# One-core transformer block kernel: the compressed branch's weight chunks spread over eight attention steps, and its later pieces moved

## What is computed

```python
def compress(kv, pos_emb, w1, w2):
    blocks = kv[:, idx] + pos_emb            # 31 blocks of 32 tokens, stride 16
    hid = jax.nn.gelu(flat @ w1)             # (31, 2048) @ (2048, 256), for keys and for values
    return hid @ w2                          # 64 columns
...
kc, vc = compress(k_cmp, ...), compress(v_cmp, ...)
kc = apply_rope(kc, ccos, csin)
p_cmp = masked_softmax(einsum(q, kc), valid_c)   # 31 compressed keys
o_cmp = einsum(p_cmp, vc)
out = gates[0] * o_cmp + gates[1] * o_slc + gates[2] * o_win
```

## Time and profile before

| what | value |
|---|---|
| median of 3 runs | 2398.99 us (2395.02 to 2399.94) |
| the profiled execution's own time | 2396.53 us |
| its span in the profile | 2394.7 us |
| share of the span, PE busy | 97% |
| share of the span, DVE busy | 64% |
| share of the span, ACT busy | 38% |
| the attention steps in the profile | 183.94 to 309.55 us |
| step 4, 16, 28 and 36 begin on PE at | 205.21, 230.67, 264.27 and 285.86 us |

### The profile page before, as it was taken

One profiled execution on the slowest core, in us unless ns is written; L12 is line 12 of the kernel. 1 busy time (PEld: TensorE's weight loads), 2 busy tenths in 40 slices (PEclk: granted clock), 3 DMA queues, 4 the chain that ended last, 5 costly groups with the idle time before them and its releaser, 6 DMA issues.

```text
span 2394.7 us, 29589 instructions
## 1 busy us (share of the span) xinstructions
PE 2319.8 (97%) x11200; PEld 1945.8 (81%) x11200; DVE 1525.8 (64%) x2596; ACT 915.8 (38%) x1329; POOL 845.3 (35%) x620
## 2 busy tenths in 40 slices
PE   7989899999999999999999999999999999999996
PEld 6878888888888887788888888888888888888884
DVE  4366667777435766567977764552222788888887
ACT  4336544333325445333323333443222333333332
POOL 0030011221000000000057787886760766666651
PEclk9999999999999999999999999999999999999998
DMA  6222046786332221233366665559676999999993
GB/s 211 77 65 62 1 158 226 268 276 206 105 97 80 88 71 53 93 127 97 118 155 146 146 144 131 119 121 279 146 204 233 324 368 353 343 357 364 358 352 130
DMA packets 205115, 434.21 MB, mean 181 GB/s; under 512 B 54112, under 2 KB 104304, under 8 KB 204464
## 3 DMA queue, kind: packets, MB, share of 16 engines
q1 hardware_dynamic: 81840, 251.79, 30.9%
q0 software_dynamic: 72368, 119.73, 18.5%
q10 hardware_dynamic: 50768, 60.82, 7.4%
HBM read 369.22 MB, written 63.05 MB: 181 GB/s over the span
## 4 chain that ended last, share of the span: by engine, by line
PE 93%; DVE 3%; ACT 1%; DMA 1%; issue 1%; POOL 0%; SPq 0%; DVEq 0%; ACTq 0%
PE PS L266 28%; PE PS L267 28%; PE PS L268 28%; PE PS L2228 1%; PE PS L2328 1%; PE PS L2160 1%; PE PS L410 1%; PE PS L2080 1%; PE PS L2148 1%; PE PS L2306 1%; DMA RAW<-in_w_in 1%; PE PS L2005 1%; DVE PS L1878 0%; DMA RAW<-in_peer_v 0%; PE PS L2014 0%
## 5 line engine op out<-in xcount | busy, mean ns | idle before, releaser
L261 DVE TENSOR_TENSOR WL<-RAW,WH 128x1024 fp32r<-128x1024 f32 (+1 forms) x414 | 505.9, 1223 | 588.1 <-ACT WH L255 558.3
L266 PE MATMUL PS<-HH,WH 128*128 128x512 f32 x1696 | 667.2, 393 | 5.9 <-DVE HL L435 4.3
L268 PE MATMUL PS<-HH,WL 128*128 128x512 f32 x1696 | 660.9, 390 | 0.0
L267 PE MATMUL PS<-HL,WH 128*128 128x512 f32 x1696 | 660.7, 390 | 0.0
L861 POOL DMA_INDIRECT gates<-A,PLACE x256 | 436.7, 1706 | 330.7 <-DVE PLACE L1809 204.9
L255 ACT ACTIVATE WH<-RAW 128x1024 fp32r<-128x1024 f32 (+1 forms) x414 | 434.8, 1052 | 255.2 <-PE PS L268 223.0
L266 PEld LDWEIGHTS PS<-HH,WH 128*128 128x128 f32 x1696 | 318.9, 188 | 73.8 <-issue 5.7
L268 PEld LDWEIGHTS PS<-HH,WL 128*128 128x128 f32 x1696 | 318.6, 188 | 66.6
L267 PEld LDWEIGHTS PS<-HL,WH 128*128 128x128 f32 x1696 | 319.0, 188 | 65.5 <-issue 1.0
L266 PE MATMUL PS<-WH,WGH 128*128 128x512 f32 x768 | 299.1, 389 | 4.6 <-DVE WGL L1862 3.9
L267 PE MATMUL PS<-WL,WGH 128*128 128x512 f32 x768 | 298.8, 389 | 0.0
(11 more groups left out here) (351 smaller groups left out, 2747.8 us busy)
## 6 DMA issues: line engine op xcount, KB each, us to landing
RAW<-in_peer_u SPq DMA_DIRECT2D x128, 512.0 KB
RAW<-in_peer_v SPq DMA_DIRECT2D x128, 512.0 KB
A<-in_w_ada POOLq DMA_DIRECT2D x48, 512.0 KB, 4.6
A<-gates ACTq DMA_DIRECT2D x32, 768.0 KB
A<-acts ACTq DMA_DIRECT2D x32, 768.0 KB
RAW<-in_ffn_up SPq DMA_DIRECT2D x44, 512.0 KB
gates<-A POOLq DMA_DIRECT2D x16, 1024.0 KB, 6.8
acts<-GATE SPq DMA_DIRECT2D x64, 256.0 KB
```

What stands on the lines that cost most here:

```text
L261: nc.vector.tensor_tensor(WLr[:, slot(c), 0:w], RAW[:, slot(c), 0:w], WH[:, slot(c), 0:w], ALU.subtract).then_inc(sem("low_done"), 1)
L266: nc.tensor.matmul(out, L[0], R[0], start=first, stop=False)
L267: nc.tensor.matmul(out, L[0], R[1], start=False, stop=False)
L268: return nc.tensor.matmul(out, L[1], R[0], start=False, stop=last)
```

## The change

The chunks of w1 are taken one in each of steps 0 to 7 in place of two in each of steps 0 to 3. The pieces of the chain behind them move: the hidden layer's by four steps (square from 4 to 8, and so on up to the product with w2 from 10 to 14 and the rope from 11 to 15), the transpose of the keys from 13 to 16, KCT from 14 to 17, and everything behind it by three steps. The first group's output is taken in step 8 beside the second's, in place of step 4. No instruction is added or removed.

```diff
+        def taken_at(s):
+
+            ends = [u for u in range(len(units)) if ends_group(u)]
+            return ends[0:2] if s - 3 == ends[1] else [s - 3] if s - 3 in ends[2:] else []
+
...
-        CS_AT = (15, 16, 17, 18, 20, 21, 22, 23)
-        CS_TAKEN_AT = (19, 24)
-        PTC_AT = (30, 32)
-        CO_AT = (34, 36, 38, 40)
+        CS_AT = (18, 19, 20, 21, 23, 24, 25, 26)
+        CS_TAKEN_AT = (22, 27)
+        PTC_AT = (33, 35)
+        CO_AT = (37, 39, 41, 43)
 
         def chunks_at(s):
 
-            return [2 * s, 2 * s + 1] if s < 4 else []
+            return [s] if s < 8 else []
...
-                if s == 4:
+                if s == 8:
                     act.wait_ge(sem("chunk_used"), FIRST["cmp"] + 8)
                     nc.scalar.activation(HU, PS[0:64, 6, :], ACT.Square).then_inc(sem("hidden_act"), 1)
-                if s == 6:
+                if s == 10:
...
-                if s == 26:
+                if s == 29:
                     act.wait_ge(sem("late_shifted"), 1)
                     nc.scalar.activation(E4, E4, ACT.Exp).then_inc(sem("late_exp"), 1)
...
-                if s == 5:
+                if s == 9:
                     dve.wait_ge(sem("hidden_act"), 1)
...
-                if s == 7:
+                if s == 11:
...
-                if s == 9:
+                if s == 13:
                     dve.wait_ge(sem("mlp_made"), 1)
...
-                if s == 11:
+                if s == 15:
                     dve.wait_ge(sem("mlp_made"), 2)
...
-                if s == 14:
+                if s == 17:
                     dve.wait_ge(sem("mlp_made"), 3)
...
-                if s == 25:
+                if s == 28:
                     dve.wait_ge(sem("cs_taken"), 2)
...
-                if s == 27:
+                if s == 30:
                     dve.wait_ge(sem("late_exp"), 1)
...
-                if s == 28:
+                if s == 31:
...
-                u = s - 3
-                if u >= 0 and ends_group(u):
+                for u in taken_at(s):
...
-                if s == 8:
+                if s == 12:
                     pe.wait_ge(sem("hidden_dve"), 3)
...
-                if s == 10:
+                if s == 14:
                     pe.wait_ge(sem("mlp_kept"), 1)
...
-                if s == 13:
+                if s == 16:
                     pe.wait_ge(sem("mlp_kept"), 2)
```

More of the change, by code:

```diff
@@ L1483, in _ @@
                         .then_inc(sem("cmp_probs"), 1)
-                if s == 29:
+                if s == 32:
                     dve.wait_ge(sem("late_exp"), 2)
```

## The result

The changed kernel takes 2422.72 us in the median of 10 runs (2404.24 to 2429.57), the kernel before 2394.86 us in 10 runs (2393.44 to 2399.94): ratio 1.0099, 95% interval 1.0081 to 1.0118. It is slower by 1.0% (the two medians by themselves are 1.2% apart), four times what was forecast, and above the range. It also spreads over 25 us where the kernel before spreads over 6. The profiled execution is one of the quicker ones, 2415.28 us, span 2413.5, mean granted clock 0.982 (before: 0.991).

The account below looks back on a forecast made before the run. The prediction took PE, with 93% of the chain of waits, as the bound. Added waits of +4.55 us and +1.5 for the clock gave +6.0 on the profiled execution, thus a 2405.0 us median, 0.25% slower; range 2397.5 to 2410.

Parts of the forecast that it names:

- (8): PE's clock: a slow restart after the new 2.9 us wait, other waits up to 1.7 us hardly counting; +1.5 us.
- Rival D: Clock costs more: slow restarts last longer or recur around steps 31, 33, 35; +9 us, 2408 us, chance 0.16.
- (1): Chunks, one a step: PE's wait for the low part of chunk 7 goes; -1.7 us.
- (2): Both takes in step 8: new wait in step 9, +0.35 us; hidden-layer wait 1.1 for 0.3, +0.8 us.
- (3): Copies of the hidden values, step 13: no take stands ahead there, so the wait shrinks; -0.7 us.
- (4): Keys' transpose in step 16, right after the rope in step 15: a new PE wait; +1.0 us.
- (5): KCT behind a norm in step 17, compressed scores in step 18: a new PE wait; +1.8 us.
- (6): Softmax in steps 28 to 32: waits of 5.95 us against 3.7, including 3.7 for the probabilities; +2.25 us.
- (7): Outputs in steps 37, 39, 41, 43: second waits 2.9 us, last two 0.35 each; +0.75 us.
- Rival C: Not slower: probabilities ready when PE asks in step 33; 2396 to 2400 us, put at 2398, chance 0.12.
- steps 16, 18 and 39: Expected PE waits: 1 to 2 us each at keys' transpose and first compressed scores, nearly 3 at the second output.
- the longest wait at the first transposes: Expected sign: PE's longest wait stands at the first transposes of the probabilities, over 3 us.

Follow-up runs that it names:

- e1: The changed kernel with KCT made ahead of the retention norm on VectorE in step 17; 2400.34 us, ratio 1.0014 to the kernel before.
- e2: As e1, with PE also transposing the keys in step 17 in place of 16; 2400.66 us, ratio 1.0012 to the kernel before.
- e8: The changed kernel, waits kept, with 32 filler matmuls (128x256) on PE in step 20; 2409.76 us, ratio 1.0056 to the kernel before.
- e4: The kernel before with only the change's later half (keys' transpose, KCT, compressed scores, softmax, outputs moved); 2425.50 us, ratio 1.0093.
- e9: e2 with probabilities' transposes and outputs later, and chunks, hidden layer and first take as in the kernel before; 2396.12 us, ratio 0.9997.
- e10: The kernel before with 9 and 16 filler matmuls ahead of its two waits for the probabilities; 2393.65 us, ratio 0.9991.
- e12: The kernel before, nothing moved, with one added PE wait in step 18 for the exponent of unit 18; 2406.46 us, ratio 1.0047.
- e3: The changed kernel with 14 filler matmuls on PE in step 18 ahead of the kept wait for KCT; 2401.79 us, ratio 1.0026 to the kernel before.
- e5: e2 with the compressed outputs in steps 37, 40, 42, 44 in place of 37, 39, 41, 43; 2399.38 us, ratio 1.0008 to the kernel before.
- e7: e2 with probabilities' transposes and outputs in later steps, and 16 filler matmuls ahead of the probabilities in step 34; 2396.73 us, ratio 0.9995.

## Why the prediction was wrong

The direction was right, and the places. The step that failed is (8), the clock, which was put at +1.5 us and measured some +24: 148.30 x 0.17 = 25.2 us lost in the stage, against 125.61 x 0.01 = 1.3 before. (The prediction's "1.3 us at most" is this rounded figure; the one window of the earlier trace rows alone gives 1.56.) Its own sentence "the other waits of up to 1.7 us bring hardly anything" read the kernel before, where a wait of that length lies in the chunk steps (256-column products behind it), as a price for every place. At step 18 the same length brings the clock down. And I took the length of a slow stretch from the one that was there to see, 4 us; behind step 18 it was 38, and it is the length, not the fall, that costs. Rival D had the mechanism, that restarts may last longer, and priced it at 9 us from the same one row.

Point by point, the waits: (1) as said, the wait for chunk 7 is gone. (2) half: no wait in step 9 can be seen (0.35 was expected; VectorE began the first take at 210.37 us, right behind the maximum of step 8, for it waits only for group 0's own last product, long done), and L2095 waits 0.7 for the 1.1. (3) 0.2, as said. (4) 1.0, as said. (5) 1.7 for 1.8. (6) 3.7 for the probabilities as said, but only once the clock is whole (e1, e2); in the changed kernel, 1.4. (7) 2.9, then 0.3 and 0.3, as said. In clock-weighted time the stage did not grow by the 4.5 us of the sum but stayed level, since on a slow PE waits for VectorE shrink (1.4 us in place of 3.7 for the probabilities). e2, where the long stretch is absent, is the nearest to what the sum described, and by ratio 0.12% slower.

Rival C (the probabilities are ready when PE asks) came half true in a way that helped nothing: PE was late at half clock. The changed profile's signs in the prediction were right for steps 16, 18 and 39, wrong for "the longest wait at the first transposes" and for "some 6 us longer" (22.7).

The Trainium skill ("TensorE: Matmul & The Clock Gate", Part 1, "What's actually happening") says that activity releases the throttle. The runs agree in part: in e8 the clock came back under a burst of 32 products, but in the changed kernel it stayed at 0.50 with PE busy in 32.00 of 32.00 us.

What stays open: why the wait of 1.75 us for chunk 7 brought the clock down in none of the five profiles that have it (before, e4, e9, e10, e12), while 1.4 us at step 18 did in e12, and waits of some 0.46 and 0.81 us close together did in five of nine; what decides it from run to run; and what in the stream of PE ends a stretch. The wide chunk products behind the former wait are a likely difference, which was not tried.

## What to carry to other kernels

Don't take the price of a wait of PE from another place in the kernel. Here 1.75 us ahead of the chunk products cost its length in every profile, while 1.4 us in step 18 cost some eight times its length in the median, and differently from run to run. When a kernel's times spread and span times mean clock doesn't, look for the window in which the clock is 0.50, then for the wait at its head; two moved instructions (e1), or fillers over the wait (e3), may give it back. A chain of small steps that is moved by whole steps meets other neighbours in the queue of the slower engine, so list what stands ahead of each piece there before choosing the step.

## What was not expected of the hardware

At 0.50 the clock stayed for 32 us with PE busy in 32.00 of them (the changed kernel), and for over 50 in e4 (0.52 over 56 us). In e8, with 32 products of 256 columns on end, it came back within the window of 16 us; in e4 it stayed at 0.50 through nine such products in threes. In the profiles of the changed kernel, e3, e5, e7 and e8 it fell behind two waits of 0.45 to 0.48 and 0.81 us. By its times one program (e4) met the long stretch in nine of 12 runs and missed it in three, a spread of 36 us.
